# Order of roots and pair sums, and sums of weight quarters by accumulating DMAs in a two-stage transformer kernel

## The reference, cut to what matters

```
def rms_norm(x, g):
    y = x * rsqrt(mean(x * x, axis=-1) + 1e-6)
    return y * g

def sq_relu_mlp(h, w_up, w_down):          # twice: 1024 -> 4096 -> 1024
    return square(relu(h @ w_up)) @ w_down

# last layer: gated feed-forward, 1024 -> 2816 -> 1024, then the final norm
a, b = split(rms_norm(x, g) @ w_ffn_in)
x = x + (silu(a) * b) @ w_ffn_out
return rms_norm(x, norm_final)
```

## Time and profile before

| | |
|---|---|
| runs | 1855.75, 1854.32, 1854.08 us; median 1854.32 |
| profiled execution | 1855.39 us |
| its span, first to last instruction | 1854.1 us |
| TensorE matmul (PE) busy | 1809.6 us, 98% |
| TensorE weight load (PEld) busy | 1463.9 us, 79% |
| VectorE (DVE) busy | 1301.1 us, 70% |
| ScalarE (ACT) busy | 797.7 us, 43% |
| GpSimd (POOL) busy | 282.8 us, 15% |
| mean granted TensorE clock | 0.989 of full |
| DMA | 174.98 MB, 94 GB/s, 27.6% of 16 engines by SyncE's queue, 1.1% by GpSimd's |

### The profile page before, as it was taken

How to read it: one execution, slowest core, us unless ns; L and a number is a source line. 1 busy time by engine, 2 the same in 40 slices (tenths; PEclk the granted TensorE clock), 3 DMA queues, 4 the chain that set the end, 5 groups by cost and what they waited for, 6 DMA issues and landing times.

```text
span 1854.1 us, 21884 instructions
## 1 busy us (share of the span) xinstructions
PE 1809.6 (98%) x8584; PEld 1463.9 (79%) x8584; DVE 1301.1 (70%) x1694; ACT 797.7 (43%) x1046; POOL 282.8 (15%) x227
## 2 busy tenths in 40 slices
PE   9999899999999999899999989999999999999998
PEld 7788688888877668688888868788787888788886
DVE  7885878686879865677786857766446446856757
ACT  6743434343444863334343344555323333323324
POOL 0004000000145864000000051111001321001010
PEclk9999899999999999999999989999999999999999
DMA  6233150522233103341405022221332324331411
GB/s 229 91 114 113 46 161 30 173 91 91 64 97 121 40 4 111 113 140 43 159 25 180 21 80 81 79 68 60 95 97 89 104 69 159 100 127 47 148 57 57
DMA packets 146374, 174.98 MB, mean 94 GB/s; under 512 B 7296, under 2 KB 120064, under 8 KB 146272
## 3 DMA queue, kind: packets, MB, share of 16 engines
q1 hardware_dynamic: 144256, 166.45, 27.6%
q0 software_dynamic: 2016, 7.14, 1.1%
HBM read 171.31 MB, written 2.14 MB: 94 GB/s over the span
## 4 chain that ended last, share of the span: by engine, by line
PE 85%; DVE 5%; issue 4%; ACT 3%; POOL 2%; DMA 0%; SPq 0%; DVEq 0%; POOLq 0%; ACTq 0%
PE bank L968 26%; PE bank L970 26%; PE bank L969 26%; PE bank L1004 1%; PE bank L1183 1%; DVE wlo L1995 1%; PE bank L1209 1%; ACT whi L1447 1%; DVE XC L2092 1%; PE bank L1320 1%; PE bank L1338 1%; POOL Hw L952 1%; DVE rstd L2011 1%; PE bank L1187 1%; POOL wlo L772 0%
## 5 line engine op out<-in xcount | busy, mean ns | idle before, releaser
L968 PE MATMUL bank<-Ahi,whi 128*128 128x512 f32 x1400 | 552.0, 394 | 12.4 <-DVE wlo L1995 5.8
L970 PE MATMUL bank<-Ahi,wlo 128*128 128x512 f32 x1400 | 546.1, 390 | 0.0
L969 PE MATMUL bank<-Alo,whi 128*128 128x512 f32 x1400 | 546.0, 390 | 0.0
L1995 DVE TENSOR_TENSOR wlo<-stage,whi 128x2048 fp32r<-128x2048 f32 (+1 forms) x133 | 306.4, 2304 | 158.6 <-ACT whi L1447 158.5
L1447 ACT ACTIVATE whi<-stage 128x2048 fp32r<-128x2048 f32 (+1 forms) x139 | 262.6, 1889 | 228.5 <-PE bank L970 203.1
L968 PEld LDWEIGHTS bank<-Ahi,whi 128*128 128x128 f32 x1400 | 262.9, 188 | 78.2 <-DVE wlo L1995 8.0
L970 PEld LDWEIGHTS bank<-Ahi,wlo 128*128 128x128 f32 x1400 | 262.8, 188 | 56.3
L969 PEld LDWEIGHTS bank<-Alo,whi 128*128 128x128 f32 x1400 | 263.0, 188 | 55.3 <-issue 1.2
L968 PE MATMUL bank<-whi,Hh 128*128 128x512 f32 x602 | 238.2, 396 | 15.9 <-issue 13.8
L969 PE MATMUL bank<-wlo,Hh 128*128 128x512 f32 x602 | 236.5, 393 | 0.0
L970 PE MATMUL bank<-whi,Hl 128*128 128x512 f32 x602 | 236.4, 393 | 0.0
(11 more groups left out here) (358 smaller groups left out, 2467.3 us busy)
## 6 DMA issues: line engine op xcount, KB each, us to landing
stage<-in_mlp_w_up SPq DMA_DIRECT2D x32, 1024.0 KB, 5.4
stage<-in_w_in SPq DMA_DIRECT2D x22, 1024.0 KB, 5.1
stage<-in_w_ffn_in SPq DMA_DIRECT2D x22, 1024.0 KB, 4.9
quad<-in_mlp_w_down SPq DMA_DIRECT2D x16, 1024.0 KB, 6.1
stage<-in_mlp_w_down SPq DMA_DIRECT2D x16, 1024.0 KB, 4.9
stage<-in_rec_w_in SPq DMA_DIRECT2D x6, 1024.0 KB, 5.3
stage<-in_att_w_in SPq DMA_DIRECT2D x6, 1024.0 KB, 5.3
stage<-in_rec_w_out SPq DMA_DIRECT2D x4, 1024.0 KB, 5.7
```

The source lines that it names most:

```text
L968: e.matmul(ps, hi, rh, start=first, stop=False, skip_group_check=onto)
L969: e.matmul(ps, hi, rl, start=False, stop=False, skip_group_check=onto)
L970: return e.matmul(ps, lo, rh, start=False, stop=last, skip_group_check=onto)
L1995: e.tensor_tensor(lo_of(u)[:, 0:nk, 0:n], source(u), f32(hi_of(u)[:, 0:nk, 0:n]), ALU.subtract).then_inc(s_lo[slot_of[u]], 1)
```

## The change

The change has four parts.

1. The order of the seven products is B11, B21, T1, B22, T2, T3, T4, and the operands T1 to T4 are sums in place of differences (T1 = q11 + q12, T2 = T1 + q22, T4 = T2 + q21, T3 = q12 + q22). The signs move into the left operands and into `add_sum`. The sums are made by DMAs from GpSimd's queue that read a quarter from DRAM and add it onto the quarter in SBUF (`sum_quarters`). Each waits until the sum before it has been split, T3 only until q12 has landed. `difference` is gone from VectorE.
2. The root matmul stands after the first product of its layer (`m == 0`). In the up-projections `first_of_pair`, `second_of_pair`, `high_sums` and `low_sums` stand at other places between the `relu`s and the splits, and each `relu` of the third and fourth pair stands ahead of fewer of them. Loads of q12 and q11 go out behind two units of the next up-projection instead of one.
3. Ahead of the gated linear attention ScalarE scales all eight blocks first and squares them behind that. The root matmuls use banks 6 and 7 and stand behind the first of K's two products. The split of Q, K and V stands ahead of the root on ScalarE and VectorE.
4. At the end of the kernel the row sums are kept per half row, GpSimd multiplies six of the eight half rows by the norm's column weights, and ScalarE scales four of them that VectorE scaled before.

```
-RIGHT = ["B11", "B21", "T1", "T2", "B22", "T3", "T4"]
-LEFT = [0, 1, 4, 5, 6, 3, 2]
-BANK = ["p", "q", "r", "p", "r", "p", "p"]
+RIGHT = ["B11", "B21", "T1", "B22", "T2", "T3", "T4"]
+LEFT = [0, 1, 4, 6, 5, 3, 2]
+BANK = ["p", "q", "r", "r", "p", "p", "p"]
...
             if g:
-                up_loads(n[0])
-                slab_loads(("dn", l, g), "q11", "q12")
-                up_loads(*n[1:])
+                up_loads(*n[:2])
+                slab_loads(("dn", l, g), "q12", "q11")
+                up_loads(*n[2:])
...
+        def sum_quarters(key, name):
+            if name == "T3":
+                e.wait_ge(*t_load[key, "q12"])
+            else:
+                e.wait_ge(*split_done((*key, {"T1": "B11", "T2": "T1", "T4": "T2"}[name])))
+            e.dma_start(quadrant(key, HOME[name]), slabs[key][{"T1": "q12", "T2": "q22", "T4": "q21", "T3": "q22"}[name]],
+                        accum_op=ALU.add).then_inc(summed(key, name)[0], 16)
+
+        def mlp_sums(l):
+            for g in range(4):
+                for name in ("T3", "T1", "T2", "T4"):
+                    sum_quarters(("dn", l, g), name)
...
         e.wait_ge(*ring.free(("root", 0)))
+        mlp_sums(0)
...
-            follows = {3: 0, 4: 2, 5: 3, 6: 5}
+            follows = {3: 2, 4: 0, 5: 4, 6: 5}
...
         def slab(key, fresh, after, end=None):
             lo(u + 2)
             low_sums(pair_no(key) + units[u] - 1)
-            difference(key, "T2")
...
             for r in range(1, 5):
                 lo(u + r + 2)
                 add_sum(key, r, 0, fresh)
                 add_sum(key, r, 1, fresh)
-                if r == 2:
-                    difference(key, "T4")
...
                 for mm in range(4):
                     if mm:
                         relu(l, 8 * g + 2 * mm - 1)
-                        if mm > 1:
-                            for u in w[mm][:-1]:
-                                lo(u)
+                        first_of_pair(q0 + mm - 1, (s_q, n0 + 2 * mm - 1))
+                    if mm > 1:
+                        low_sums(q0 + mm - 2)
+                    for u in w[mm]:
+                        lo(u)
+                    if mm == 0 and g == 0:
+                        root(("root", l), f"mlp{l}")
+                    relu(l, 8 * g + 2 * mm)
+                    if mm:
                         second_of_pair(q0 + mm - 1, (s_q, n0 + 2 * mm))
-                        lo(w[mm][-1])
-                        if mm > 1:
-                            difference(key, ("T1", "T3")[mm - 2])
-                        low_sums(q0 + mm - 1)
-                    else:
-                        lo(w[0][0])
-                        if g == 0:
-                            root(("root", l), f"mlp{l}")
-                    relu(l, 8 * g + 2 * mm)
-                    first_of_pair(q0 + mm, (s_q, n0 + 2 * mm + 1))
+                first_of_pair(q0 + 3, (s_q, n0 + 7))
+                low_sums(q0 + 2)
                 relu(l, 8 * g + 7)
                 second_of_pair(q0 + 3, (s_q, n0 + 8))
...
         def for_gla(n, m):
             scaled_hi(m, gfm[:, m:m + 1])
-            if n == 7:
-                hi(u_of["lr"] + 1)
-            for i, (acc, t, kw) in enumerate(...):
-                ...
+            if n < 7:
+                return
+            for n, m in enumerate(TURN):
+                for i, (acc, t, kw) in enumerate(...):
+                    ...
         mlp(1, for_gla)
-        hi(u_of["Q", 0] + 1)
-        e.wait_ge(*ring.full("ss"))
+        hi(u_of["K", 0])
+        hi(u_of["V", 0])
+        e.wait_ge(s_ss, 1)
```

More of the change, by code:

```diff
@@ L313, in stage_for @@
             return stage_of[u]
-        return stage_of[u_of[(*u, {"q21": "T4", "q22": "B22"}[name])]] if name in ("q21", "q22") else None
+        return stage_of[u_of[(*u, {"q21": "B21", "q22": "B22"}[name])]] if name in ("q21", "q22") else None
     loaded, t_load = [0, 0], {}
@@ L348, in quadrant, with summed @@
         return wide(quad[name == "q12"] if s is None else stage[s], n)
-    HOME = {"B11": "q11", "T1": "q11", "T2": "q11", "T3": "q12", "B21": "q21", "T4": "q21", "B22": "q22"}
+    HOME = {"B11": "q11", "T1": "q11", "T2": "q11", "T4": "q11", "T3": "q12", "B21": "q21", "B22": "q22"}
+    def summed(key, name):
+        if name == "T3":
+            return s_acc[1], 16 * slab_no[key] + 16
+        return s_acc[0], 48 * slab_no[key] + {"T1": 16, "T2": 32, "T4": 48}[name]
     def source(u):
@@ L463, in ring_ffn @@
         for j in range(0, FG[g][1], 2):
-            pair(("fg", g, j), ("fg", g, j), ("fg", g, j + 1))
+            ring.add(("fg", g, j))
             if g == 0 and j == 0:
                 ring.add("root_f")
+            pair(("fg", g, j), ("fg", g, j + 1))
             pair(("fu", g, j), ("fu", g, j), ("fu", g, j + 1))
@@ L711, in load @@
             elif before is not None:
[L712 to L715, removed]
+                key = before[0]
+                e.wait_ge(*split_done((*key, {"q11": "T4", "q12": "T3", "q21": "B21", "q22": "B22"}[before[1]])))
             if name is not None:
@@ L953, in gpsimd_program @@
                                 ALU.mult).then_inc(s_fu, 1)
+            for name in ("T2", "T4") if g else ("T3", "T1", "T2", "T4"):
+                sum_quarters(("fd", g), name)
+        e.wait_ge(s_cols, 32)
+        for i, (j, h) in enumerate(LAST):
+            e.wait_ge(s_ysq, i + 1)
+            e.tensor_tensor(sum_of(j, h), sum_of(j, h), fin2b[:, h * 512:h * 512 + 512], ALU.mult).then_inc(s_yw, 1)
     def tensor_program(e):
@@ L1265, in tensor_program @@
         product(("qk", 2), s, 128, Ahi, Alo)
[L1266 to L1270, removed]
         s = take_unit(("K", 0))
         product(("qk", 1), s, 0, Ahi, Alo)
+        e.wait_ge(s_tsp, 14)
+        e.matmul(banks[6][:, :], ones[:, :], sqa_e[:, :], start=True, stop=True).then_inc(s_ss, 1)
+        e.matmul(banks[7][:, :], ones[:, :], sqb_e[:, :], start=True, stop=True).then_inc(s_ss, 1)
         product(("qk", 3), s, 128, Ahi, Alo)
@@ L1415, in ffn_up @@
                     turn_x(1, 0, 1)
+                    root("root_f", "ffn")
                 product(("fg", g, j + 1), s, 128, Ahi, Alo)
@@ L1439, in hi @@
                 else:
[L1440 removed]
+                    e.wait_ge(*summed(key, name))
             else:
@@ L1949, in scalar_program @@
                 if g == 0 and j == 0:
-                    for x in range(4, 8):
-                        keep_x(x)
+                    keep_x(4)
+                    keep_x(5)
                     std_of("root_f", 1024)
+                    keep_x(6)
+                    keep_x(7)
                 gate_root(g, j)
@@ L1980, in scalar_program @@
+        last_square(1, 1, 0, 1)
+        last_square(2, 0, 1, 4)
+        last_square(3, 1, 1, 4)
+        e.wait_ge(s_ysq, 4)
+        for j in range(2):
+            last_root(j)
+        last_square(4, 2, 1, 5)
+        last_square(5, 3, 1, 5)
+        for j in range(2):
+            last_scale(j, 0).then_inc(*st.inc())
+            last_scale(j, 1).then_inc(s_yg, 1)
+        for j in range(2, 4):
+            last_square(4 + j, j, 0, 6)
             e.wait_ge(s_ysq, 5 + j)
-            e.wait_ge(s_yb, j + 1)
@@ L2487, in vector_program @@
         mlp(1, lambda n, m: scaled_lo("gla", m, gfm[:, m:m + 1], n))
[L2490 to L2491 removed]
+        lo(u_of["Q", 0])
+        lo(u_of["K", 0])
+        lo(u_of["V", 0])
         e.wait_ge(s_std, 1)
[L2493 to L2496 removed]
+        e.tensor_scalar(sqt2[:, :], banks[6][:, :], 1e-6 / 1024, 1e-12, ALU.mult, ALU.add).then_inc(s_ssr, 1)
+        e.wait_ge(s_ss, 2)
+        e.wait_ge(s_ssr, 1)
+        e.scalar_tensor_tensor(sqb_e[:, :], banks[7][:, :], 1.0 / 1024, sqt2[:, :], ALU.mult, ALU.add).then_inc(s_ssr, 1)
         e.wait_ge(s_std, 2)
```

180 lines of the change are left out of this document (81 added, 99 removed).

## The result

The changed kernel took 1918.87 us (median of 4 runs, 1917.07 to 1919.4) against 1854.2 us for the one before: ratio 1.0345, interval 1.0327 to 1.0363. It is 64.7 us slower. Forecast were 1841 us and, for 8 in 10, a range of 1826 to 1905. The first rival, the late sums, had given 1916.

The account below looks back on a forecast made before the run. TensorE, its matmuls busy for 98% of the span, was taken as the bound. 1855.4 − 27.4 of gains + 14.4 for the sums = 1842.4, or 1841 against the median; own range 1831 to 1852, 8 in 10 1826 to 1905.

Parts of the forecast that it names:

- The first rival: Sums land late, L = 8.4: slabs lose 61.7 us plus 18 to 36 of clock, time 1916; chance 0.34.
- L = 4.9 + 0.9 = 5.8: Time in us from issue to landing of a 1 MB sum: plain SyncE load plus what GpSimd's queue adds.
- the delay L − 5.0: MLP slabs, fourth product (B22's): waits for the add_sum behind T2's split; 0.8 us each, 6.4 over eight slabs.
- the bound of 6.7: Value of L from which the sums' losses reach the gains, so that the first rival decides.
- the 13.5 us of 2 MB loads: GpSimd's loads, two in flight, as many bytes as one sum reads if it reads its target too; bound from above.
- L − 6.5: MLP slabs, sixth product: delay by the add_sum behind T4's split, counted only where positive; forecast 0.
- T1 and T3 have over 15 us of room: In the slabs, these two sums cause no delay, as B11 is split three products before the slab starts.
- Ahead of the gated attention: K comes 4 to 7 us late, clock may fall once: 8.2 us lost instead of 11.2, gain 3.
- Rival 4: K's wait eats its stage: ten additions at 3.3 us lose 10 more, 1851 to 1854; chance 0.08 with rival 3.
- the gains at the first slabs: First slab of each MLP: TensorE's waits and half clock go, as relu comes earlier; 10.8 and 9.6 us.
- rival 3: B11's stall isn't the relu's: 6.7 + 6.7 and 4.4 us of clock stay, 1859; chance 0.08 with Rival 4.
- the end: After the last matmul: VectorE's last addition waits less, ScalarE has four more scalings; gain 0.5, between −1 and 1.5.

Follow-up runs that it names:

- experiment 3: Changed kernel, but in the last layer's first slab the sums T3 and T1 are issued ahead of GpSimd's last two multiplications: 1905.14 us.
- experiment 8: As run 7, but VectorE sums T1 and T3 too, so no accumulating DMA is left: 1840.27 us.
- run 7: Changed kernel with T2 and T4 summed by VectorE, last layer's first sums ahead of GpSimd's last multiplications, K's unit rounded after ten squares: 1824.74 us.
- experiment 5: Changed kernel, add_sum of places 2 and 5 ahead of splits, last layer's first sums before GpSimd's last multiplications, K rounded after ten squares; sums still DMAs: 1843.48 us.

## Why the prediction was wrong

**The step that failed is "I take L = 4.9 + 0.9 = 5.8".** It measured 9.0, and experiment 2, which leaves out the adding alone, takes back 69.4 of the 77.9 us between forecast and result. The chain built on L was right: the delay L − 5.0 at the fourth product gives 4.0, and eight waits of 3.6 to 4.1 us were measured, each released by the `add_sum` that was named. I took for the nearest row a plain load of the same bytes into `stage`. The sums go into `quad`, and the trace of the kernel before has a row for that too, which I left out:

```profile
quad<-in_mlp_w_down SPq DMA_DIRECT2D x16, 1024.0 KB, 6.1
```

With it the same sum gives L = 7.0, past the bound of 6.7 at which losses reach gains. (These loads go out in pairs; the first of a later pair landed in 5.1 to 5.9 us.) And a transfer that reads its target too has no row of its kind in the trace; the 13.5 us of 2 MB loads counted the bytes rightly, and I used them only as the far end. The queue's part, 4.5 against 3.6, was fair: without the adding the landing took 5.4. The bound of 6.7 lay barely above my value; with bounds of 4.9 and 13.5 that asked for better odds for the rival than 0.34.

**The clock.** In the forecast the stalls of the MLPs were too short to lower it. At waits of 3.6 to 4.1 us it fell in each MLP slab, for 3.4 us, and these waits became steps of 5.1 to 5.8. The same half clock fits the sixth product, which waited for 0.6 to 1.8 us and not for L − 6.5 = 2.5: TensorE came to it 1.7 us later by what the clock had cost, and T4's sums landed 8.6 to 10.0 us after their issue. The first rival had both, and its 88.7 us (61.7 + 27) stand against 90.1 measured. That the sums agree so well is in part luck: it had too much at the sixth product (15.2 us without the clock, 11.0 measured) and too little in the last layer (19.3 us and its stalls' clock, 35.9 measured).

**The last layer's first slab.** "T1 and T3 have over 15 us of room" was wrong for g = 0, where the code issues both sums behind all the multiplications, as the account of the change itself says: T1's left at 1620.0, TensorE wanted its product at 1628.0. The sum, second in the queue, landed 12.9 us after its issue. That cost 13.7 us (experiment 3), and would have cost some at any L: with plain loads T1's product still waited for 3.8 us.

**Ahead of the gated attention** the forecast's mechanism came true at a higher price: the stage lost 11.8 us (11.2 + 0.6) and not 8.2. I forecast K 4 to 7 us late and one fall of the clock. It was 8.3 us late, 2.2 of them because its split took 4.47 us beside the additions in place of 2.29. The clock fell once and stood at half for 10.2 us, in 5.9 of which TensorE worked, so that cost 2.9 us. Rival 4's mechanism did not come: the additions took 1.29 us in the median, not 3.3. The stage's loss ate what part 3 gained.

```profile
1133.20:1143.40 10.20, 5.87 (x14) 4.61 (x15) 6.48 (x2) 1.58 (x1) 4.26 (x7) 0.50 0.49 157
```

**Right:** the gains at the first slabs (10.8 and 9.6, measured 11.1 and 10.1) with their reason: no gap is left at B11, against rival 3, and the `relu` ran at 206.13, where I had placed it. In experiment 8, where a wait of 0.77 us is back in B11's product, the profile names a `relu`, that of product 7, as its end. Product 6's `relu` in the changed kernel:

```profile
206.13 0.69 DVE L2244 SCALAR_TENSOR_TENSOR ht<-bank,rstd 128x512 f32<-128x512 f32 x1
```

Right too were the end, and that differences off VectorE win next to nothing where they were hidden: in the seven products of each of the six MLP slabs behind the first ones, run 7 is 0.1 us faster than the kernel before. (Put back into the new order, the sums cost 0.7 to 0.8 us a slab, experiment 8.)

## What to carry to other kernels

Work that moves from an engine to an accumulating DMA turns from a short instruction into a latency: 2.3 us on VectorE became 9.0 us here. It pays where the result is wanted long after (T1 and T3 by DMA were worth 15.5 us), and costs where it stands in a chain (T2 and T4); a change can be split along that line. And when data come late, look first at what stands behind them in an in-order queue: edits of order alone (experiment 5) took 75 us off the changed kernel with every transfer kept.

## What the runs showed of the hardware

An accumulating DMA of 1 MB from DRAM onto SBUF took the DMA engines 2.05 times the time of a plain one (95 against 47 us of engine time per MB, experiment 2) and landed in 9.0 against 5.4 us; its instruction held GpSimd for 1.28 us, the plain one's for 0.75. Its packets had 2048 bytes, those of the plain one 4096. Of two issued 0.8 us apart the first landed after 8.6 us and the second after 12.9.

Beside GpSimd's additions of 128x512, which took 1.3 us alone, a split of VectorE that took 2.29 us alone took 3.30 us in one place and 4.47 in another, and the addition beside the first took 3.33. Both engines paid.
